# Sample rows of the linear attention: spread queries as stationary operand on four column groups, state updates on alternating row groups

## What is computed

```
o_inter = (q * exp(b)) @ S            # 4 query rows of each sample against that sample's state
o_intra = A @ v                       # 4x4 causal scores inside the sample
k_dec   = k * exp(b_last - b)
S_new   = exp(b_last) * S + k_dec^T @ v
```

## Time and profile before

| | |
|---|---|
| time of 3 runs, median (lowest to highest) | 2615.33 us (2611.34 to 2617.35) |
| span of the profiled execution | 2614.3 us |
| mean granted TensorE clock in it | 0.981 |
| TensorE matmuls busy | 2492.0 us, 95% |
| VectorE busy | 1620.1 us, 62% |
| ScalarE busy | 1148.0 us, 44% |
| the four turns with samples | about 300 to 602 us of the span |

### The profile page before, as it was taken

The page is one execution under the profiler, slowest core; times in us unless marked ns, Lnnn a source line. Parts: engine busy times, 40 slices in busy tenths (PEclk is TensorE's granted clock), DMA queues, the critical chain, the costliest instruction groups (busy, mean ns, idle before and its releaser), DMA issues. The chain is left out here.

```text
span 2614.3 us, 37791 instructions
## 1 busy us (share of the span) xinstructions
PE 2492.0 (95%) x15455; PEld 2181.2 (83%) x15455; DVE 1620.1 (62%) x2921; ACT 1148.0 (44%) x1810; POOL 44.1 (2%) x66
## 2 busy tenths in 40 slices
PE   7999999999999999999998899989999999999997
PEld 5777989887888889999997677767788889999996
DVE  5677566576666556765756655564766556655556
ACT  4655444443443334343335766653434334322333
POOL 0000000000000000000000000000000000000000
PEclk9999999989999999999999999989999999999998
DMA  4222223223434332422323242222343332332222
GB/s 156 65 73 89 81 70 105 89 91 103 160 109 125 103 95 88 131 81 90 112 83 90 95 125 62 84 77 70 99 131 96 113 97 94 100 114 81 94 85 96
DMA packets 83129, 255.18 MB, mean 98 GB/s; under 512 B 12499, under 2 KB 30076, under 8 KB 81020
## 3 DMA queue, kind: packets, MB, share of 16 engines
q1 hardware_dynamic: 63884, 202.43, 24.4%
q0 software_dynamic: 5792, 28.05, 3.3%
q10 hardware_dynamic: 13280, 22.28, 2.6%
HBM read 225.92 MB, written 26.74 MB: 97 GB/s over the span
## 5 line engine op out<-in xcount | busy, mean ns | idle before, releaser
L441 PE MATMUL banks<-act_hi,w_lo 128*128 128x272 f32 (+1 forms) x2952 | 977.4, 331 | 13.9 <-DVE act_lo L2256 6.7
L441 PE MATMUL banks<-act_hi,w_hi 128*128 128x272 f32 (+1 forms) x2952 | 963.0, 326 | 0.0
L441 PE MATMUL banks<-act_lo,w_hi 128*128 128x272 f32 (+1 forms) x2952 | 961.6, 326 | 0.0
L419 ACT ACTIVATE w_hi<-w_raw 128x1024 fp32r<-128x1024 f32 x366 | 380.7, 1055 | 695.8 <-PE banks L464 486.4
L424 DVE TENSOR_TENSOR w_lo<-w_raw,w_hi 128x1024 fp32r<-128x1024 f32 x366 | 443.2, 1223 | 367.0 <-ACT w_hi L419 366.7
L441 PEld LDWEIGHTS banks<-act_hi,w_lo 128*128 128x128 f32 x2952 | 561.3, 190 | 73.0 <-issue 20.7
L441 PEld LDWEIGHTS banks<-act_lo,w_hi 128*128 128x128 f32 x2952 | 562.4, 191 | 43.3 <-issue 1.7
L441 PEld LDWEIGHTS banks<-act_hi,w_hi 128*128 128x128 f32 x2952 | 560.9, 190 | 44.2
L476 DVE TENSOR_TENSOR acc<-acc,banks 128x272 f32<-128x272 f32 (+1 forms) x624 | 315.3, 520 | 194.3 <-PE banks L464 190.9
L464 PE MATMUL banks<-h_hi,w_lo 128*128 128x272 f32 (+1 forms) x1056 | 345.4, 327 | 20.8 <-DVE acc L476 12.9
L464 PE MATMUL banks<-h_hi,w_hi 128*128 128x272 f32 (+1 forms) x1056 | 343.7, 325 | 0.0
(11 more groups left out here) (234 smaller groups left out, 2646.8 us busy)
## 6 DMA issues: line engine op xcount, KB each, us to landing
w_raw<-wall SPq DMA_DIRECT2D x366, 512.0 KB, 3.6
normed<-h_scratch POOLq DMA_DIRECT2D x20, 352.0 KB, 4.1
h_scratch<-acc POOLq DMA_DIRECT2D x3, 2176.0 KB, 7.9
h_scratch<-acc POOLq DMA_DIRECT2D x3, 2048.0 KB, 8.0
gstates<-state ACTq DMA_DIRECT2D x4, 1024.0 KB, 6.4
gla_s<-gstates ACTq DMA_DIRECT2D x4, 1024.0 KB, 6.5
bias<-bias_scratch ACTq DMA_DIRECT2D x28, 128.0 KB, 2.9
bias_scratch<-bias_rows ACTq DMA_DIRECT2D x8, 383.0 KB
```

Of the source, the lines that this page charges most:

```text
L419: nc.scalar.activation(WH[:, b % RING], WR[:, b % RAW], ACT.Copy).then_inc(w_hi, 1)
L441: last = nc.tensor.matmul(PS[:, bank, 0:n], w, a[X][:, k, o:o + n], start=(k == 0 and first), stop=(k == KT - 1 and w is wh and a is AH))
```

## The change

The queries of the samples are spread into `QSP`: for each sample a block of 32 columns that is zero except for 4 columns with its queries. That block (128x32) becomes the stationary operand and the state (128x256) the moving one, on the column group `b % 4`; two samples accumulate in one group. The values' part is one more matmul into column group 0. The result is token-first in four groups of 32 partitions; ScalarE copies it to `XS`, and two matmuls with a stacked identity `SEL` add the groups and bring it back feature-first (`sample_outputs_by_feature`). That step stands after the second half of the key projection; ScalarE's copy to `O` moves behind its own key step. The samples' keys and values are kept four times, on all 128 partitions, so that `sample_deltas` can take row group `b % 4`.

```diff
-        KDM = place("gkd_masked", [SAMP, NB, P], offset=OH0_AT)
+        KDM = place("gkd_masked", [P, 2, P], offset=OH0_AT)
+        KREP = place("gkd_four_times", [P, P], offset=OH0_AT + 1024)
...
+        QSP = place("gq_spread", [P, NB * (SAMP + LS)])
+        VREP = place("gv_four_times", [P, 2, P])
+        XS = place("go_by_token", [P, DV])
+        SEL = place("select", [P, SAMP])
...
+        def four_times(x):
+            return x.unsqueeze(1).broadcast_to([P, 4, SAMP])
...
+                    if X:
+                        for d in range(2):
+                            last = nc.tensor.transpose(PS[:, 2, d * P:(d + 1) * P], VREP[:, d], ident[:])
...
-                        last = nc.tensor.transpose(PS[0:SAMP, 3, P:2 * P], KTl[1][:, HP:HP + SAMP], ident[:])
+                        last = nc.tensor.transpose(PS[:, 3, P:2 * P], KREP[:], ident[:])
...
                 def sample_outputs():
                     pe.wait_ge(s_upd, 4 * u + 4)
                     pe.wait_ge(si_in, 16 * h + 16)
+                    for b in range(NB):
+                        j = 32 * (b % 4)
+                        nc.tensor.matmul(PS[j:j + SAMP, 0, 0:DV], QSP[:, b * SAMP:(b + 1) * SAMP], SB[:, b],
+                                         start=(b < 4), stop=(4 < b), skip_group_check=True)
+                    nc.tensor.matmul(PS[0:SAMP, 0, 0:DV], AT[0:SAMP, HP:HP + SAMP], V[0:SAMP, HB, :],
+                                     start=False, stop=True, skip_group_check=True).then_inc(xs_full, 1)
+
+                def sample_outputs_by_feature():
+                    pe.wait_ge(xs_ev, h + 1)
                     for d in range(2):
-                        nc.tensor.matmul(PS[:, d, 0:SAMP], V[0:SAMP, HB, d * P:(d + 1) * P], AT[0:SAMP, HP:HP + SAMP],
-                                         start=True, stop=False, skip_group_check=True)
-                    for b in range(NB):
-                        x = b * LS
-                        for d in range(2):
-                            last = nc.tensor.matmul(PS[:, d, x:x + LS], SB[:, b, d * P:(d + 1) * P],
-                                                    QT[1][:, HP + x:HP + x + LS], start=False, stop=(b == NB - 1),
-                                                    skip_group_check=True)
+                        last = nc.tensor.matmul(PS[:, d, 0:SAMP], XS[:, d * P:(d + 1) * P], SEL[:], start=True, stop=True)
                     last.then_inc(os_full, 1)
...
-                        nc.tensor.matmul(PS[:, 6 + b % 2, 0:DV], KDM[:, b], V[0:SAMP, HB, :],
+                        j = SAMP * (b % 4)
+                        nc.tensor.matmul(PS[:, 6 + b % 2, 0:DV], KDM[j:j + SAMP, b // 4], V[j:j + SAMP, HB, :],
                                          start=True, stop=True).then_inc(ss_full, 1)
...
                 if more:
                     key(u + 1, SECOND)
+                if X:
+                    sample_outputs_by_feature()
                 outputs(2)
...
+            nc.vector.memset(QSP[:], 0.0).then_inc(qs_zero, 1)
-            dve.wait_ge(m0c_in, 16 * 4)
+            dve.wait_ge(m0c_in, 16 * 11)
...
-                nc.vector.tensor_tensor(KTl[1][:, 0:W], K[:, 0:W], T1[:, 0:W], ALU.mult).then_inc(in_k, 1)
-                nc.vector.tensor_tensor(QT[1][:, 0:W], Q[:, 0:W], QT[1][:, 0:W], ALU.mult).then_inc(in_q, 1)
+                if X:
+                    nc.vector.tensor_tensor(KREP[:].rearrange("p (j s) -> p j s", j=4), four_times(K[:, HP:WM]),
+                                            four_times(T1[:, HP:WM]), ALU.mult)
+                nc.vector.tensor_tensor(KTl[1][:, 0:HP], K[:, 0:HP], T1[:, 0:HP], ALU.mult).then_inc(in_k, 1)
+                if X:
+                    dve.wait_ge(qs_zero, 1)
+                    if h:
+                        dve.wait_ge(xs_full, h)
+                    nc.vector.tensor_tensor(QSP[:].rearrange("p (b s) -> p b s", b=NB)[:, :, 0:LS],
+                                            Q[:, HP:WM].rearrange("p (b s) -> p b s", b=NB),
+                                            QT[1][:, HP:WM].rearrange("p (b s) -> p b s", b=NB), ALU.mult)
+                nc.vector.tensor_tensor(QT[1][:, 0:HP], Q[:, 0:HP], QT[1][:, 0:HP], ALU.mult).then_inc(in_q, 1)
...
-                    nc.vector.tensor_tensor(KDM[:], KDS[:].unsqueeze(1).broadcast_to([SAMP, NB, P]), bc(BMASK[:], P),
+                    nc.vector.tensor_tensor(KDM[:], KDS[:].unsqueeze(1).broadcast_to([P, 2, P]), bc(BMASK[:], P),
                                             ALU.mult).then_inc(kdm, 1)
...
+                    if o + w_ > HP:
+                        last = nc.scalar.activation(VREP[:, t].rearrange("p (j s) -> p j s", j=4),
+                                                    four_times(PS[:, 2 * t + c, w_ - SAMP:w_]), ACT.Copy)
...
                 kept(0)
                 if X:
-                    act.wait_ge(os_full, h + 1)
-                    nc.scalar.activation(O[:, :, HP:WM], PS[:, 0:2, 0:SAMP], ACT.Copy).then_inc(os_ev, 1)
+                    act.wait_ge(xs_full, h + 1)
+                    nc.scalar.activation(XS[:], PS[:, 0, 0:DV], ACT.Copy).then_inc(xs_ev, 1)
                 for step in gla_steps(ACT_GLA, u, "outputs"):
                     act_step(act, *step, 0)
                 if more:
                     key(u + 1)
+                if X:
+                    act.wait_ge(os_full, h + 1)
+                    nc.scalar.activation(O[:, :, HP:WM], PS[:, 0:2, 0:SAMP], ACT.Copy).then_inc(os_ev, 1)
                 kept(1)
...
-            for dst, src in ((MLEV, masks), (SMASK, smask), (BMASK, bmask), (SCM, scanm[:, :, HP:HP + WM])):
+            for dst, src in ((MLEV, masks), (SMASK, smask), (SCM, scanm[:, :, HP:HP + WM])):
                 sp.dma_start(dst[:], src).then_inc(m0c_in, 16)
+            for j in range(4):
+                x = slice(j * SAMP, (j + 1) * SAMP)
+                sp.dma_start(BMASK[x], bmask[:, j:NB:4], allow_slow_non_contiguous=True).then_inc(m0c_in, 16)
+                sp.dma_start(SEL[x], ident_in[0:SAMP, 0:SAMP]).then_inc(m0c_in, 16)
```

More of the change, by code:

```diff
@@ L248, in build @@
         S = place("gstate", [P, H, DV])
-        KDS = place("gkd_s", [SAMP, P])
+        KDS = place("gkd_s", [P, P])
         SB = place("gstates", [P, NB, DV])
@@ L253, in build @@
         SMASK = place("smask_t", [SAMP, SAMP], bf16)
-        BMASK = place("bmask_t", [SAMP, NB])
+        BMASK = place("bmask_t", [P, 2])
+        QSP = place("gq_spread", [P, NB * (SAMP + LS)])
+        VREP = place("gv_four_times", [P, 2, P])
+        XS = place("go_by_token", [P, DV])
+        SEL = place("select", [P, SAMP])
         EL = place("gel", [P, 16])
@@ L338, in build @@
         os_full, os_ev, ss_full, ss_upd = (sem(x) for x in ("os_full", "os_copied", "sstate_full", "sstate_updated"))
+        qs_zero, xs_full, xs_ev = (sem(x) for x in ("q_spread_zeroed", "os_by_token_full", "os_by_token_copied"))
         gq_sq, gq_f, gq_ss, gq_ms, gq_rs, gq_si, gq_o, gq_h, gq_l = (
@@ L721, in by_token @@
                         pe.wait_ge(ms_done, NORMS[SUMS_AT[u]])
-                    for i in range(HB + X):
-                        n = CH if i < HB else SAMP
+                    for i in range(HB):
                         for d in range(2):
-                            last = nc.tensor.transpose(PS[0:n, i // 2, (i % 2) * DV + d * P:(i % 2) * DV + (d + 1) * P],
-                                                       O[:, d, i * CH:i * CH + n], ident[:])
+                            last = nc.tensor.transpose(PS[:, i // 2, (i % 2) * DV + d * P:(i % 2) * DV + (d + 1) * P],
+                                                       O[:, d, i * CH:(i + 1) * CH], ident[:])
+                    if X:
+                        for d in range(2):
+                            last = nc.tensor.transpose(PS[:, 2, d * P:(d + 1) * P], VREP[:, d], ident[:])
                     last.then_inc(vt_full, 1)
@@ L1148, in values @@
                     act.wait_ge(v_full_, VR[u, t, c])
-                    nc.scalar.activation(O[:, t, o:o + w_], PS[:, 2 * t + c, 0:w_], ACT.Copy).then_inc(v_ev_, 1)
+                    last = nc.scalar.activation(O[:, t, o:o + w_], PS[:, 2 * t + c, 0:w_], ACT.Copy)
+                    if o + w_ > HP:
+                        last = nc.scalar.activation(VREP[:, t].rearrange("p (j s) -> p j s", j=4),
+                                                    four_times(PS[:, 2 * t + c, w_ - SAMP:w_]), ACT.Copy)
+                    last.then_inc(v_ev_, 1)
             def values_done(u, t):
@@ L1192, in turn @@
                 if X:
-                    last = nc.scalar.activation(V[0:SAMP, HB], PS[0:SAMP, 2, 0:DV], ACT.Copy)
+                    last = nc.scalar.activation(V[:, HB], PS[:, 2, 0:DV], ACT.Copy)
                 last.then_inc(vt_ev, 1)
@@ L1210, in turn @@
                 if X:
-                    last = nc.scalar.activation(KDS[:], PS[0:SAMP, 3, P:2 * P], ACT.Copy)
+                    last = nc.scalar.activation(KDS[:], PS[:, 3, P:2 * P], ACT.Copy)
```

## The result

The changed kernel takes 2590.34 us (median of 4 runs, 2589.46 to 2591.08); the kernel before, beside it, 2615.18 us. The ratio is 0.9901, 95% interval 0.9885 to 0.9918. The profiled execution spans 2588.6 us against 2614.3, and the mean granted clock rose from 0.981 to 0.988.

What follows compares the result with a forecast made beforehand. TensorE, busy 95% of the span, was taken as the bound. Savings of 15.8 + 3.35 + 6.25 - 0.2 = 25.2 us bring the span from 2614.3 to 2589.1, so a median of 2590 us, range 2580 to 2603.

Steps and rivals of the forecast that it cites:

- Block, keys, way back: Turns 4 to 6, sample block through return to feature-first: 10.35 us become 1.6 + 3.0 + 0.5 = 5.1 us.
- Rival C: Sample block and increments: four column groups don't overlap, 2.64 us more a turn; 2606 us, chance 0.04.
- The clock: Key half after the sample block, turns 4 to 6: low clock goes with the 4-column passes; projection takes 3.0 us.
- rival A: After the sample block in turns 4 to 7: the low clock stays, 15.4 us lost; 2605 us, chance 0.14.
- E: Sample block and keys: groups run one after another and keep the clock low, 6.7 us a turn slower; 2642 us, chance 0.03.
- Strict order (B): Sample block and increments: passes start strictly in program order, 7.9 us lost; 2598 us, chance 0.12.
- Pairs: State increments: an L782 matmul pair falls from 1.06 to 0.63 us; 3.35 us arrive in turns 4 to 6.
- D: Before the output projection: VectorE's chain takes the increments' gain, `go_lo` comes no earlier; 2599 us, chance 0.06.
- the wait of turn 5: Turn 5, second increment pair: a new TensorE wait of 1.0 us for the first two updates, leaving 0.45 us gain.
- Turn 7: Turn 7, sample block to output projection: 2.05 + 6.8 + 1.7 - 0.55 - 2.1 - 1.65 = 6.25 us saved.
- Turns 4 to 6 together: Sample block to output projection in three turns: 15.8 us from block and keys plus 3.35 from increments.
- VectorE, ScalarE, SyncE: Added copies and loads on other engines: `KREP` loses 0.2 us in turn 7; wider copies and seven constant loads cost nothing.

Runs made afterwards that it cites:

- one-group run: Changed kernel with all eight samples in the first column group, so no two passes lie side by side; 2600.37 us, ratio 0.9940.
- cut 4-column block: Kernel before with its sample block in turns 4 to 6 cut in two around the first 12 key passes; 2614.73 us, ratio 0.9992.
- column half: Changed kernel with state increments, their keys, values and masks as in the kernel before; 2599.27 us, ratio 0.9938.
- row-group half: Changed kernel with sample outputs in 4-column passes as in the kernel before and no spread queries; 2607.01 us, ratio 0.9964.

## Why the prediction was right, point by point

*Block, keys, way back.* 10.35 us became 5.01 (342.22 to 347.23); 5.1 was predicted. That four groups run side by side, which no row had shown, is shown by the one-group run (3.57 against 1.00). Rival C is out.

*The clock.* It stayed up in turns 4 to 6, in both profiles; rival A is out, and E with it. The reason given, narrow passes rather than work on part of the array, fits: the one-group block keeps 1.00, and the cut 4-column block keeps it in two turns of three. But each 4-column pass also loads a new stationary operand of 128 columns, where the new passes load 32; no run separates the few moving columns from that load.

*Strict order (B).* The block is as long with each group's passes in a row. By the rule of the Trainium skill (TensorE: Matmul & The Clock Gate, Part 3, what overlaps and what doesn't) it would have taken 2.9 us, an estimate of 13 steps of 0.22; the measured 1.02 decides against the rule for column groups.

*Pairs, and D.* A pair costs 0.63 as predicted. I said 1.45, 0.45 and 1.45 us after VectorE's chain; the column half alone puts them at 1.24, 0.65 and 1.24. The sum, 3.1, is close to 3.35, but the shares are not: the chain takes a little more, and the wait of turn 5 was mis-sized at 1.0 us. I had the second pair wait for both updates, but its first matmul needs only the first of them. It waited 0.40 us, the row is 0.99 us long instead of 0.70, and turn 5 is 0.61 us longer than turn 4. D was right that the chain becomes the bound, by 0.1 to 0.2 us, and wrong that it takes all.

*Turn 7.* 6.25 us predicted from block to projection, 6.98 measured between the first two profiles, with shares that moved: the new low stretch that I charged with 1.65 did not come (it came in one other execution), the `XS` wait was 0.47 (0.55), the wait for `O` 1.80 (2.1), and the pairs gave 0.08 for 1.7. That the two terms missed by some 1.6 us each, in opposite directions, is luck. Against the second profile of the kernel before, the turn gives only 3.8. The term that took half of a 13.6 us low stretch as saved rests on one execution: in the other the stretch was 6.8 us long (the second profile's).

```profile
577.10:583.90 6.80, 6.80 (x21) 4.75 (x19) 0.97 (x3) 6.53 (x6) 0.00 (x0) 0.50 0.00 0
```

*Turns 4 to 6 together:* 19.0 us by the table, 19.15 predicted. Here the profiles agree to 0.1 us, and this is what carries the forecast.

*VectorE, ScalarE, SyncE.* `KREP` cost 0.17 us in turn 7's way to its keys (0.2 predicted): the wait for `gkt` is 2.02 us, against 1.85 before and 1.85 in the column half, which makes no `KREP`. The other copies and the seven loads bring no new wait of TensorE. The copies that now fill 128 partitions were put at nothing; on ScalarE that of the values takes 0.03 us more than on 32, and the wait behind the keys' copy grew from 0.83 to 0.85 us (group by line and form, 300 to 620 us):

```profile
L1225 ACT ACTIVATE gv<-banks 128x256 f32<-128x256 f32 x4 | 1.6, 392 | 0.0
```

*What was given back.* Behind turn 7 nothing was changed, yet that part ranges from 2011.1 to 2017.3 us over the profiles, with no order by kernel. The row-group half and the kernel before, each in its second profile, from the projection of turn 7 to the end:

```profile
593.30:2604.40 2011.10, 1924.96 (x12114) 1692.94 (x12112) 1231.52 (x2276) 849.91 (x1401) 34.56 (x49) 0.99 0.31 99
```

```profile
598.32:2615.60 2017.28, 1933.57 (x12114) 1699.01 (x12112) 1231.77 (x2276) 848.82 (x1401) 34.46 (x49) 0.98 0.31 99
```

The same 12114 matmuls keep TensorE busy for 8.6 us more, at a lower mean clock. The 0.9 us that the changed kernel's first profile lost there lie at 606.35, where it waited 2.16 us for `w_lo`, against 1.25 before and 1.21 in its second profile.

Between the turns it is alike. Ahead of turn 6 TensorE waits 3.1 us for `acc` in both profiles of the changed kernel, but only in the second is the clock low behind it (the first profile's stretch, then the second's), and there turns 5 and 6 lie 1.6 us further apart.

```profile
453.70:457.10 3.40, 3.37 (x27) 3.37 (x28) 3.40 (x6) 0.00 (x0) 0.16 (x1) 1.00 1.05 436
```

```profile
453.70:457.10 3.40, 3.40 (x16) 3.40 (x16) 3.40 (x7) 0.00 (x0) 0.00 (x0) 0.50 1.04 441
```

The forecast knew nothing of these parts; that it meets the median within 1 us is partly luck.

## What to carry to other kernels

Price a block of narrow passes together with what runs behind it: here 3.4 of 10.35 us were the clock's (6.8 us at half speed), and wide moving operands took it away even where the array was three quarters unused. When a stage shortens, look at once for the next in line; here VectorE's chain was 0.16 us behind and left 1.24 us of the pairs' 1.72 in turns 4 and 6. And take a second profile of the kernel before when a term rests on a stretch of low clock: turn 7's differed by 3.2 us between two executions.

## What the runs showed of the hardware

Four float32 column groups work as independent lanes here: 16 passes of 256 columns take 1.00 us on four groups and 3.57 on one, in whichever of two orders they are written. A float32 run of 32 passes with 4 columns is followed by 3.4 to 6.8 us at clock 0.50 in turns 4 to 6; 16 passes of 256 columns on a quarter of the columns, 3.57 us long, are followed by none. The start of that stretch in turn 4 repeats to 0.2 us between executions of one kernel and lies 2.1 to 2.4 us apart between two kernels with the same block at the same place, which no run here explains. The same wait of 3.1 us was followed by 3.4 us at clock 0.50 in one execution of the changed kernel and by none in another.
